# Fused reference block: attention logits from halves stacked on 128 rows by GpSimd

## What is computed

```python
# first attention: 16 heads of 64, three groups of dilated windows, softmax, weights per group
logits = jnp.einsum('bqhd,bqkhd->bhqk', q_blk, k_sel).astype(jnp.float32) + bias   # masked outside the window
lse = jax.nn.logsumexp(logits, axis=-1)
o = jnp.einsum('bhqk,bqkhd->bqhd', jnp.exp(logits - lse[..., None]), v_sel)
# second attention: 8 pairs of heads of 64, values of 128
logits = jnp.einsum('bqhjd,bkhjd->bhjqk', q_blk, k).astype(jnp.float32) + bias[None]
p = jax.nn.softmax(logits, axis=-1)
a = p[:, :, 0] - lam_full * p[:, :, 1]
o = rms_norm_2(jnp.einsum('bhqk,bkhe->bqhe', a, v), subln_g) * (1.0 - lambda_init)
```

## Time and profile before

| | us |
|---|---|
| median of three runs | 3872.05 |
| the profiled execution's own time | 3869.35 |
| its span, first to last instruction | 3867.6 |
| TensorE busy (matmul records) | 3714.9 |
| VectorE, ScalarE, GpSimd busy | 2274.2, 1322.8, 1401.8 |
| first attention, first to last logit record | 2549.4 to 2708.1 |
| second attention, first to last logit record | 3284.7 to 3411.5 |
| mean granted clock of TensorE | 0.979 |

### The profile page before, as it was taken

How to read it: one execution, slowest core, us unless ns; L and a number is a source line. 1 busy time by engine, 2 the same in 40 slices (tenths; PEclk the granted TensorE clock), 3 DMA queues, 4 the chain that set the end, 5 groups by cost and what they waited for, 6 DMA issues and landing times.

```text
span 3867.6 us, 48582 instructions
## 1 busy us (share of the span) xinstructions
PE 3714.9 (96%) x16460; PEld 2915.3 (75%) x16460; DVE 2274.2 (59%) x3647; ACT 1322.8 (34%) x1818; POOL 1401.8 (36%) x596
## 2 busy tenths in 40 slices
PE   6999899899999999999999999999999999989998
PEld 4787787678888888878888887854688877358886
DVE  5786996145767575177777775335564431657541
ACT  4554323334443434321111113246422232653221
POOL 2211443333333333344444443410244434124442
PEclk8999999999999999999999999989999999999999
DMA  5435222233545454675566652221122223112222
GB/s 200 147 110 195 92 93 77 76 97 118 169 155 184 139 187 136 214 253 183 182 185 187 186 179 94 93 67 42 55 98 95 96 87 102 58 43 93 94 97 76
DMA packets 266641, 486.58 MB, mean 126 GB/s; under 512 B 16721, under 2 KB 148177, under 8 KB 266097
## 3 DMA queue, kind: packets, MB, share of 16 engines
q1 hardware_dynamic: 81936, 299.93, 24.3%
q10 hardware_dynamic: 184580, 184.95, 14.7%
HBM read 415.48 MB, written 84.02 MB: 129 GB/s over the span
## 4 chain that ended last, share of the span: by engine, by line
PE 92%; DVE 3%; ACT 2%; issue 1%; DMA 1%; POOL 0%; DVEq 0%; SPq 0%; ACTq 0%; POOLq 0%
PE ps L354 26%; PE ps L355 26%; PE ps L356 26%; PE ps L575 3%; PE ps L650 3%; PE ps L668 2%; PE ps L658 1%; DMA ring<-panels 1%; PE ps L450 1%; PE ps L386 1%; PE ps L555 0%; PE ps L381 0%; DVE sq L1352 0%; DVE arena L1452 0%; ACT arena L1174 0%
## 5 line engine op out<-in xcount | busy, mean ns | idle before, releaser
L1951 POOL TENSOR_TENSOR ring_r<-ring,high_w 128x1024 fp32r<-128x1024 f32 x552 | 1366.1, 2476 | 2248.2 <-ACT high_w L763 1763.1
L354 PE MATMUL ps<-uT_r,high_w 128*128 128x512 f32 x2624 | 1046.2, 399 | 24.8 <-POOL ring_r L1951 11.9
L356 PE MATMUL ps<-uT_r,ring_r 128*128 128x512 f32 x2624 | 1026.5, 391 | 0.0
L763 ACT ACTIVATE high_w<-ring 128x1024 fp32r<-128x1024 f32 x440 | 464.3, 1058 | 1292.4 <-PE ps L356 1150.5
L355 PE MATMUL ps<-sq_r,high_w 128*128 128x512 f32 x2048 | 798.7, 390 | 0.0
L355 PE MATMUL ps<-part,high_w 128*128 128x512 f32 x1856 | 735.1, 396 | 0.0
L354 PE MATMUL ps<-part,high_w 128*128 128x512 f32 x1664 | 670.1, 403 | 13.7 <-issue 6.5
L356 PE MATMUL ps<-part,ring_r 128*128 128x512 f32 x1664 | 658.7, 396 | 0.0
L354 PEld LDWEIGHTS ps<-uT_r,high_w 128*128 128x128 f32 x2624 | 496.4, 189 | 133.0 <-issue 19.9
L356 PEld LDWEIGHTS ps<-uT_r,ring_r 128*128 128x128 f32 x2624 | 495.4, 189 | 104.3
L355 PEld LDWEIGHTS ps<-sq_r,high_w 128*128 128x128 f32 x2048 | 385.7, 188 | 79.3 <-issue 1.9
(11 more groups left out here) (288 smaller groups left out, 3777.6 us busy)
## 6 DMA issues: line engine op xcount, KB each, us to landing
ring<-panels SPq DMA_DIRECT2D x568, 512.0 KB, 3.5
gdram<-arena ACTq DMA_DIRECT2D x16, 2048.0 KB, 10.6
arena<-gdram ACTq DMA_DIRECT2D x128, 256.0 KB, 5.1
arena<-adram ACTq DMA_DIRECT2D x128, 256.0 KB, 2.7
adram<-act_out ACTq DMA_DIRECT2D x112, 256.0 KB, 3.9
arena<-ada_rest ACTq DMA_DIRECT2D x32, 512.0 KB, 4.5
strips_dram<-btab ACTq DMA_DIRECT2D x4, 3584.0 KB
arena<-strips_dram ACTq DMA_DIRECT2D x32, 448.0 KB, 3.3
```

Of the source, the lines that this page charges most:

```text
L354: t_.matmul(out, wh, xh, start=(k == 0), stop=False)
L356: last = t_.matmul(out, wl, xh, start=False, stop=(k == KT - 1))
L763: s_.activation(high_w[:, j % RING], ring[:, j % RING], ACT.Copy).then_inc(hi_ready, 1)
L1951: g_.tensor_tensor(ring_r[:, j], ring[:, j], high_w[:, j], ALU.subtract).then_inc(lo_ready, 1)
```

## The change

A head's 64 rows of queries and keys are split into high (rounded) and low parts by GpSimd, ten instructions a pair in `stage_qk`. For head half hh the tile `q2` has the high part of the queries on the head's own 64 rows and their low part on the other 64; `k2` has the high part of the keys on all 128 rows (twice); `kl` has the low part of the keys on the head's own rows. A logit is then `q2` x `k2` over 128 rows (high x high + low x high) plus `q2` x `kl` over the head's 64 rows (high x low), both fp32r, added in PSUM. The tiles lie in `uT_r` and `sq_r`, which are free in an attention. After each of the ten instructions GpSimd waits for that instruction; `staged` counts ten a pair, and TensorE waits for five of them for the first head and ten for the second.

The staging of the first attention leaves ScalarE and becomes `first_attention` on GpSimd, placed in the list of low parts between the third and fourth panel of the first output projection. In the second attention the staging of the queries and keys of pair n + 2 now stands ahead of the values of pair n + 1, in place of the values of pair n + 2 behind them.

```diff
--- before.py
+++ after.py
@@ -237,8 +237,7 @@
         pb = view(12288, 2, 2, TT, T)
         strip = view(20480, 2, STRIP)
         pt = view(22272, 2, TT, T)
-        qs = sq[:, 3:5, :]
-        ks = sq[:, 5:7, :]
+        staged_in = [[uT_r[:, n, :] for n in range(5)], [uT_r[:, 5, :], uT_r[:, 6, :], uT_r[:, 7, :], sq_r[:, 3, :], sq_r[:, 4, :]]]
         vf = view(22272, 2, T)
         vs = view(26368, 2, TT, P)
         zs = slot[:, :, 0:A_HEADS * TT].rearrange("p a (b c) -> p a b c", c=TT)
@@ -644,11 +643,13 @@
                 def logit(n, par, hh, qt):
 
                     if qt == 0:
-                        pe.wait_ge(a["staged"], n * 2 + 2)
+                        pe.wait_ge(a["staged"], n * 10 + (5 * hh + 5))
                     if not (isinstance(n, int) and n * 8 + 4 * hh + qt < 4):
                         pe.wait_ge(a["nm_ready"], n * 8 + (4 * hh + qt - 3))
-                    t_.matmul(ps[:, qt, :], qs[64 * hh:64 * hh + 64, par, qt * P:(qt + 1) * P],
-                              ks[64 * hh:64 * hh + 64, par, :], start=True, stop=True).then_inc(a["lg_done"], 1)
+                    q2, k2, kl = staged_in[par][hh], staged_in[par][2 + hh], staged_in[par][4]
+                    own = slice(64 * hh, 64 * hh + 64)
+                    t_.matmul(ps[:, qt, :], q2[:, qt * P:(qt + 1) * P], k2, start=True, stop=False)
+                    t_.matmul(ps[:, qt, :], q2[own, qt * P:(qt + 1) * P], kl[own, :], start=False, stop=True).then_inc(a["lg_done"], 1)
 
                 def turn(par, src, u, qt):
 
@@ -1230,22 +1231,7 @@
                         if e == TT + 1 and n >= 2:
                             high_b(n - 2)
 
-                def stage_qk(n, par):
-
-                    sl = slice(n, n + 1) if isinstance(n, int) else bass.ds(n, 1)
-                    s_.activation(qs[:, par:par + 1, :], qT[:, sl, :], ACT.Copy).then_inc(a["staged"], 1)
-                    s_.activation(ks[:, par:par + 1, :], kT[:, sl, :], ACT.Copy).then_inc(a["staged"], 1)
-
-                def stage_v(n, par):
-
-                    vsl = slice(n * P, n * P + P) if isinstance(n, int) else bass.ds(n * P, P)
-                    s_.activation(vs[:, par], vtok[:, :, vsl], ACT.Copy).then_inc(a["v_staged"], 1)
-
-                def stage(n, par):
-                    stage_qk(n, par)
-                    stage_v(n, par)
-
-                def quarters(i, c, more=True, fetch_more=True, old=True, staging=True):
+                def quarters(i, c, more=True, fetch_more=True, old=True):
 
                     n, u = i * 2 + c // 2, i * 4 + c
                     for qt in range(TT):
@@ -1254,11 +1240,6 @@
                         if qt == 0 and old:
                             out_a(i * 2 + (c - 2) // 2, c % 2, i * 4 + (c - 2))
                         turned(c % 2, u, qt)
-                        if qt == 1 and staging:
-                            if c % 2:
-                                stage_v(i * 2 + (c + 1) // 2, (c + 1) // 2 % 2)
-                            else:
-                                stage_qk(i * 2 + c // 2 + 1, (c // 2 + 1) % 2)
                     if more and fetch_more:
                         strips(i * 4 + (c + 3), (c + 1) % 2)
 
@@ -1268,18 +1249,16 @@
                     act.wait_ge(bank_free[b], 2 * (q_qkv + 3))
                 act.wait_ge(vt_sb, 8 * s + 8)
                 if s == 0:
-                    stage(0, 0)
-                    stage(1, 1)
                     exps(0, 0, 0)
-                    quarters(0, 0, old=False, staging=False)
-                    quarters(0, 1, old=False, staging=False)
+                    quarters(0, 0, old=False)
+                    quarters(0, 1, old=False)
                     with act.Fori(0, 2) as i:
                         for c in range(2, 6):
                             quarters(i, c)
                     for c in range(2, 6):
                         quarters(2, c, fetch_more=c < 5)
-                    quarters(3, 2, fetch_more=False, staging=False)
-                    quarters(3, 3, more=False, staging=False)
+                    quarters(3, 2, fetch_more=False)
+                    quarters(3, 3, more=False)
 
                     act.wait_ge(a["lse"], 1)
                     s_.activation(zs[:, 2], zs[:, 1], ACT.Ln).then_inc(a["lse"], 1)
@@ -1950,31 +1929,70 @@
                 po.wait_ge(hi_ready, i * RING + (j + 1))
                 g_.tensor_tensor(ring_r[:, j], ring[:, j], high_w[:, j], ALU.subtract).then_inc(lo_ready, 1)
 
+            def values_in(s):
+
+                for b in range(BANKS):
+                    po.wait_ge(bank_free[b], 2 * (Q_WO_B if s else Q_WO_A))
+                po.wait_ge(vt_sb, 8 * s + 8)
+                po.wait_ge(lo_ready, 8 * ((Q_WO_B if s else Q_WO_A) - Q_HEADS) + RING - 1)
+                for n in range(2):
+                    stage_qk(att[s], n)
+                    stage_v(att[s], n)
+
+            def first_attention():
+
+                a = att[0]
+                values_in(0)
+                for n in range(6):
+                    po.wait_ge(a["lg_done"], 8 * n + 8)
+                    stage_qk(a, n + 2)
+                    po.wait_ge(a["av_done"], 2 * n + 2)
+                    stage_v(a, n + 2)
+
             def second_attention():
 
                 a = att[1]
-                for b in range(BANKS):
-                    po.wait_ge(bank_free[b], 2 * Q_WO_B)
-                po.wait_ge(vt_sb, 16)
-                for n in range(2):
-                    stage_qk(a, n)
-                    stage_v(a, n)
+                values_in(1)
                 for n in range(B_HEADS):
                     if n + 2 < B_HEADS:
                         po.wait_ge(a["lg_done"], 8 * n + 8)
+                        if n >= 3:
+                            po.wait_ge(a["oT_ready"], n - 2)
                         stage_qk(a, n + 2)
+                    if 2 <= n + 1 < B_HEADS:
+                        po.wait_ge(a["av_done"], n)
+                        stage_v(a, n + 1)
                     if n >= 2:
                         low_b(a, n - 2)
-                    if n + 2 < B_HEADS:
-                        po.wait_ge(a["av_done"], n + 1)
-                        stage_v(a, n + 2)
                 for u in (6, 7):
                     low_b(a, u)
 
             def stage_qk(a, n):
 
-                g_.tensor_copy(qs[:, n % 2, :], qT[:, n, :]).then_inc(a["staged"], 1)
-                g_.tensor_copy(ks[:, n % 2, :], kT[:, n, :]).then_inc(a["staged"], 1)
+                q0, q1, k0, k1, kl = staged_in[n % 2]
+                rows = slice(0, 64), slice(64, P)
+                done = 10 * n
+
+                def staged(ins):
+
+                    ins.then_inc(a["staged"], 1)
+                    po.wait_ge(a["staged"], done)
+
+                if n:
+                    po.wait_ge(a["v_staged"], n if a is att[0] or n < 3 else n - 1)
+                for hh in range(2):
+                    own, other = rows[hh], rows[1 - hh]
+                    q2, k2 = (q0, q1)[hh], (k0, k1)[hh]
+                    done += 1
+                    staged(g_.tensor_copy(q2[own, :], qT[own, n, :]))
+                    done += 1
+                    staged(g_.tensor_copy(k2[own, :], kT[own, n, :]))
+                    done += 1
+                    staged(g_.tensor_copy(k2[other, :], kT[own, n, :]))
+                    done += 1
+                    staged(g_.tensor_tensor(q2[other, :], qT[own, n, :], q2[own, :], ALU.subtract))
+                    done += 1
+                    staged(g_.tensor_tensor(kl[own, :], kT[own, n, :], k2[own, :], ALU.subtract))
 
             def stage_v(a, n):
 
@@ -1995,9 +2013,17 @@
                     low(at_gates + k, j)
                 po.wait_ge(og_high, k + 1)
                 g_.tensor_tensor(og_r[:, k, :], og[:, k, :], sq_r[:, k, :], ALU.subtract).then_inc(og_low, 1)
-            with po.Fori(0, at_b - at_gates - KT) as i:
+            at_a = 8 * (Q_WO_A - Q_HEADS) // RING
+            with po.Fori(0, at_a - at_gates - KT) as i:
                 for j in range(RING):
                     low(i + (at_gates + KT), j)
+            for j in range(RING - 1):
+                low(at_a, j)
+            first_attention()
+            low(at_a, RING - 1)
+            with po.Fori(0, at_b - at_a - 1) as i:
+                for j in range(RING):
+                    low(i + (at_a + 1), j)
             for j in range(RING - 1):
                 low(at_b, j)
             second_attention()
```

## The result

The changed kernel takes 3875.19 us (median of 20 runs, 3871.59 to 3878.22), the kernel before 3870.7 (20 runs, 3861.78 to 3881.98): a ratio of 1.0014, interval 1.0008 to 1.0020. That is slower by about 0.1%, within the 0.2% that the prediction calls no change; the forecast was 3851, faster. The profiled execution spans 3875.9 us against 3867.6.

A forecast was written before the change was run, and what follows sets the result against it. TensorE was taken to bound the kernel nearly everywhere. Savings of 17.1 (first attention's blocks), 0 and 0.2 (starts) and 3.5 (second attention's rounds) sum to 20.8 us, giving 3851 us, range 3834 to 3869.

The forecast's parts named there:

- The logit: Both attentions: two fp32r matmuls cost 0.60 us in place of 1.05, saving 0.45 a logit, between 0.27 and 0.60.
- First attention, steady blocks: 14 blocks with logits, weighted products and transposes: 8.96 us each against 10.18, 17.1 us saved in all.
- the 0.3 for exclusion: First attention's steady blocks: GpSimd's work delays VectorE's scale, and so the exponential and copy, by 0.3 us a block.
- The stall of 0.31 for 0.3: First attention, end of each head: the weighted matmul waits for ScalarE's last transposes copy, forecast at 0.3 us a block.
- Full value: Rival, both attentions: the switch costs nothing and VectorE's slack takes the blocking; 35 us saved, 3837 us; 22%.
- Blocking eats the gain: Rival, both attentions: GpSimd holds VectorE, blocks take 9.8 us, rounds do not shorten; 1 us saved, 3871 us; 15%.
- Staging on GpSimd: Both attentions: 10.5 us a pair, at most 4 more, copies 0.62 and subtractions 1.27; GpSimd's own time hidden.
- First attention, start: First logits up to the first block with a weighted product: zero change, between -3 and +5 us.
- Second attention, start: Up to the first statistic: first weighted product 2.9 us late, seven logits save 3.15; -0.2 us, between -4 and +4.
- Second attention, rounds 2 to 6: Each round 16.8 us against 17.52, only three logits behind ScalarE's release counting; 3.5 us saved, between 0 and 8.
- The 0.65 for exclusion: Second attention, rounds 2 to 6: a GpSimd subtraction holds VectorE's first combine, costing 0.65 us a round.
- Half clock in the rounds: Rival, second attention rounds 2 to 6: 3 us idle lowers TensorE's clock, rounds 22.7 us, total 3882, slower; 13%.

The follow-up runs named there:

- The run with 128 rows throughout: Only the first attention changed, pair 0's logits fp32 straight from queries and keys, plus the logit's second matmul zero-padded to 128 rows: 3838.84 us, ratio 0.9934.
- the two by two: Changed kernel with extra matmuls in TensorE's idle stretch of rounds, without second-attention staging of pairs 2 to 7, and with both: 3859.96, 3864.92, 3861.57 us.
- with fillers and without staging: Changed kernel with extra matmuls of constants in rounds 1 to 6 and no staging of pairs 2 to 7 in the second attention: 3861.57 us, timed once.
- the filled run: Changed kernel with seven extra matmuls of constants in each of rounds 2 to 6 of the second attention, three in round 1: 3859.96 us, ratio 0.9976.
- the run with pair 0 direct: Only the first attention changed, and in both attentions pair 0's logits are fp32 straight from queries and keys, without staging: 3845.06 us, ratio 0.9950.
- With the copy-out moved: Changed kernel with ScalarE's copy-out of the pair before placed behind the first two transposes' copies in second-attention rounds: 3859.68 us, ratio 0.9976.
- the kernel with all remedies and no fillers: Changed kernel, pair 0's logits fp32 straight from queries and keys, ScalarE's copy-out behind two transposes' copies in rounds 2 to 6: 3851.31 us, ratio 0.9958.

## Why the prediction was wrong

The forecast was 20.8 us less and the profiled executions differ by 8.3 more. Of these 29.1 us, 15.2 lie in rounds 2 to 6, 10.6 in the two starts, 1.1 in the steady blocks and the other 2.2 in the tails and outside the attentions, which were forecast at nothing (-1.6, +1.6 and +2.2).

**The logit.** Forecast 0.60 a pair, measured 0.83; the transposes ahead of it gave back 0.17 (0.36 instead of 0.53), so a quarter saved 0.39, not 0.45. The step took the 64-row matmul for one like the panels'. The run with 128 rows throughout shows what was missed: 0.55.

**First attention, steady blocks.** 8.96 forecast, 8.95 measured: luck, since the terms were off and cancelled. The quarter was 0.06 dearer, four times a block, and the 0.3 for exclusion was not felt: the scale was held up to 1.607 us, but the block from 2620.56, most of it beside 7.17 us of idle GpSimd, takes 8.95 and the next, beside its staging, 8.94. The stall of 0.31 for 0.3 is luck too. TensorE was ready 2.98 us after the logit's start and not 2.69, and the copy ended at 3.13 and not 2.87, because the new pair ends 0.22 earlier than the old logit and not 0.46. The 14 blocks gave 16.0 us in place of 17.1, since the first runs partly at half clock. The rivals Full value and Blocking eats the gain both fall here.

**Staging on GpSimd.** Right: casts 0.61 us, subtractions 1.27, with 64 rows no cheaper than the 128 of rows 6 and across the halves no dearer.

**First attention, start.** Zero forecast, 4.0 lost. The staging was right: the forecast put the first logit 7.65 us behind the last transposes (2554.0 against 2546.35 before), and it came at 7.66. The half-clock quarter was right as well, 1.45 for the pair and 0.76 for the transposes against 2.26 in all. Three terms were left out. Head 0's four logits take 5.75 us at half clock, longer than the staging of head 1 (4.9). Five logits and not four lie between there and the first weighted product, 1.4 more. And TensorE waits 1.9 us in all for ScalarE's copies, beside a VectorE that is busy 9.55 of 10 us from 2560 to 2570.

**Second attention, start.** 0.2 us were to be gained, 6.4 were lost to the first statistic. 3.4 more than forecast were lost ahead of the first weighted product: the forecast took the staging of pair 1 for what comes last there, but it was done 3.4 us before TensorE came to it, behind twelve logits at 1.45. The 3.15 that seven logits should have given back did not come: TensorE waited 1.50 us for ScalarE's copy at 3314.86, and the clock fell again 2 us ahead of the statistic.

**Second attention, rounds 2 to 6.** This is the step that decided. 16.8 us forecast, 19.86 measured. The forecast took the time ahead of ScalarE's release to be free. It isn't: work taken from TensorE there became an idle stretch of 3.3 us, the clock fell in every round, and the two by two shows at least 2.2 us a round from that. The 0.65 for exclusion measured 0.9 to 1.3. The rest is 0.55: with fillers and without staging a round takes 16.72, where the forecast's terms give 17.52 - 1.35 = 16.17. It is not settled, since the fillers may be in it. The Trainium skill, in SBUF — State Buffer (SBUF: two separate sides), has VectorE with two SBUF inputs and GpSimd shut each other out for a whole instruction. The trace agrees: a combine of 0.748 us in the median before takes up to 1.853, beside subtractions of 1.27.

The rival Half clock in the rounds had the place and the mechanism and got 13%. Its price of 22.7 was too high, since the stretch at half clock behind the release grew by some 2 us and not 4.9: from the third transposes to the statistic 4.36 us against 2.47 in the filled run.

**The evidence used against the rival** was that TensorE stayed at 1.00 from 2711 to 2723.5 with gaps. It was misread. The longest of those gaps, 2.21 us, is the last thing in that window, and rows 12 go on with 0.62 from 2723.5: the fall stands right behind it. The rival's own case cites that 0.62, so these rows spoke for the rival.

```profile
2723.54 4.57 PE L721 MATMUL ps<-cst,wg 128*128 128x128 f32 x24 [2.21 <-DVE wg L1894]
```

Open: why the clock stays low among dense logits at the starts, and why it differs between executions of the same instructions there. No run settles it. The 2.2 us outside the attentions are not explained either.

## What to carry to other kernels

Before work is taken off TensorE, ask what ends the wait behind it: if another engine's chain does, the saved time becomes idle, and the idle can cost the clock (2.2 us a round here), so leave the slower form there or fill the stretch. A new staging chain stands exposed at the start of a stage; let the first tile go the old way. When a matmul costs twice its neighbours of the same size, look at whether its weight load lies under the one before: padding to the same 128 rows was worth 13.6 us in the first attention and 14.5 in the whole here.

## What the runs showed of the hardware that was not expected

- fp32r matmuls of 512 columns that alternate 128 and 64 rows start 0.43 us apart, even in a row at full clock; with 128 rows throughout 0.23 to 0.32.
- In a row at full clock an fp32 logit costs 0.86 us, no more than the alternating pair. Its 1.05 against 0.83 came between other matmuls. From the run with pair 0 direct, the loads of two neighbouring records, of which a logit has two:

```profile
3264.24 0.19 PEld L654 LDWEIGHTS ps<-arena 64*128 64x128 f32 x1 [0.24 <-issue]
3264.67 0.19 PEld L654 LDWEIGHTS ps<-arena 64*128 64x128 f32 x1 [0.24 <-issue]
```

- At half clock the alternating pair costs 1.45 us, against 2.00 for an fp32 logit and 0.83 at full clock.
- The length of an idle stretch did not tell whether the clock fell. It fell in each round of the changed kernel, behind 2.67 to 3.32 us. With the copy-out moved it held behind 2.17 and 2.19, but in the kernel with all remedies and no fillers it fell one logit behind 2.17 and held behind 2.21. It fell once behind 0.98 us among logits, and in the first run with 128 rows once in the second attention's rounds, whose logits are fp32 and which have a single wait of 0.70 us. The same round with and without the fall:

```profile
3323.18:3342.13 18.95, 18.25 (x52) 7.15 (x51) 11.79 (x28) 14.79 (x32) 4.03 (x5) 0.92 0.16 49
...
3361.41:3378.93 17.52, 16.82 (x51) 6.65 (x50) 11.79 (x28) 13.35 (x29) 2.17 (x2) 1.00 0.08 26
```
